# Forgetting attention: one f32 score product against three products of rounded high and low parts

## The reference

```python
q = rms_norm(q.reshape(B, S, FOX_HEADS, FOX_DH), q_norm_g)
k = rms_norm(k.reshape(B, S, FOX_HEADS, FOX_DH), k_norm_g)
log_f = jax.nn.log_sigmoid(f_raw.astype(F32) + b_f.astype(F32))
c = jnp.cumsum(log_f, axis=1)
# per block of 128 queries, q scaled by Dh ** -0.5:
logits = jnp.einsum('bhtd,bshd->bhts', qb, kf) + cb[..., None] - c_t[:, :, None, :]
logits = jnp.where(key_pos[None, :] <= q_pos[:, None], logits, -jnp.inf)
probs = jax.nn.softmax(logits, axis=-1)
o = jnp.einsum('bhts,bshd->bthd', probs, vf)
```

## Time and profile before

| | |
|---|---|
| median of 3 runs | 1759.19 us (1757.87 to 1759.38) |
| span of the profiled execution | 1755.8 us |
| TensorE busy | 1687.5 us, 96% |
| its weight loads | 1287.9 us, 73% |
| VectorE busy | 882.0 us, 50% |
| ScalarE busy | 788.9 us, 45% |
| GpSimd busy | 312.6 us, 18% |

### The profile page before, as it was taken

How to read it: one execution, slowest core, us unless ns; L and a number is a source line. 1 busy time by engine, 2 the same in 40 slices (tenths; PEclk the granted TensorE clock), 3 DMA queues, 4 the chain that set the end, 5 groups by cost and what they waited for, 6 DMA issues and landing times. The chain is left out here.

```text
span 1755.8 us, 28773 instructions
## 1 busy us (share of the span) xinstructions
PE 1687.5 (96%) x11157; PEld 1287.9 (73%) x11157; DVE 882.0 (50%) x1655; ACT 788.9 (45%) x1288; POOL 312.6 (18%) x243
## 2 busy tenths in 40 slices
PE   9999999999999899799999999999999999899898
PEld 6777777777777677678777887666666665688686
DVE  5757667575666635854322200344444544577533
ACT  4746556464554722142222311556555665531411
POOL 5213212132222251300000000222221221013000
PEclk9999999999999999999989999999999999999999
DMA  6202011210102122051130202111111101051411
GB/s 158 62 26 49 13 50 22 52 37 25 50 13 57 41 97 72 13 168 46 39 110 26 71 2 45 40 45 31 46 35 42 43 22 43 2 175 40 144 46 51
DMA packets 115574, 94.42 MB, mean 54 GB/s; under 512 B 19760, under 2 KB 97776, under 8 KB 115440
## 3 DMA queue, kind: packets, MB, share of 16 engines
q1 hardware_dynamic: 115440, 92.59, 18.5%
HBM read 84.08 MB, written 8.49 MB: 53 GB/s over the span
## 5 line engine op out<-in xcount | busy, mean ns | idle before, releaser
L435 PE MATMUL gdn_unit<-part_hi,gdn_w_hi 128*128 128x512 f32 x496 | 225.7, 455 | 0.0
L437 PE MATMUL gdn_unit<-part_hi,gdn_w_lo 128*128 128x512 f32 x496 | 195.3, 394 | 0.0
L436 PE MATMUL gdn_unit<-part_lo,gdn_w_hi 128*128 128x512 f32 x496 | 194.0, 391 | 0.0
L2108 DVE CUSTOM_DVE_ANT_0 fa_probs<-fa_scores,fa_decay 128x896 f32<-128x896 f32 (+7 forms) x128 | 97.0, 758 | 120.9 <-PE fa_scores L1920 73.6
L867 DVE SCALAR_TENSOR_TENSOR x<-gdn_raw,gdn_taps,x 128x512 f32<-128x512 f32 x144 | 129.4, 899 | 24.3 <-ACT x L665 19.4
L399 POOL TENSOR_TENSOR gdn_w_lo<-ring,gdn_w_hi 128x1024 fp32r<-128x1024 f32 x31 | 75.2, 2427 | 250.7 <-ACT gdn_w_hi L645 250.7
L2054 ACT ACTIVATE fa_probs_t<-fa_turned 128x512 f32<-128x512 f32 (+1 forms) x96 | 52.3, 545 | 139.0 <-PE fa_turned L1937 138.4
L2048 ACT ACTIVATE fa_probs<-fa_probs,fa_top 128x896 f32<-128x896 f32 (+7 forms) x128 | 99.4, 777 | 22.1 <-DVE fa_top L2108 18.4
L437 PEld LDWEIGHTS gdn_unit<-part_hi,gdn_w_lo 128*128 128x128 f32 x496 | 93.1, 188 | 21.0
L435 PEld LDWEIGHTS gdn_unit<-part_hi,gdn_w_hi 128*128 128x128 f32 x496 | 93.7, 189 | 16.1 <-issue 3.6
L1295 PE MATMUL e_gate<-e_w_hi,part_hi 128*128 128x512 f32 x256 | 101.8, 398 | 3.0 <-DVE part_lo L1430 2.8
(11 more groups left out here) (329 smaller groups left out, 3681.0 us busy)
## 6 DMA issues: line engine op xcount, KB each, us to landing
ring<-in_gdn_w_in_dram SPq DMA_DIRECT2D x31, 512.0 KB, 4.1
ring<-in_ple_w_gate_dram SPq DMA_DIRECT2D x32, 256.0 KB, 3.2
ring<-in_fox_w_in_dram SPq DMA_DIRECT2D x32, 256.0 KB, 3.1
ring<-in_fox_w_in_dram SPq DMA_DIRECT2D x16, 512.0 KB, 4.7
fa_decay<-c_rows_scratch SPq DMA_DIRECT2D x64, 128.0 KB, 3.0
gdn_g_bc<-g_rows_scratch SPq DMA_DIRECT2D x8, 512.0 KB, 8.9
x_scratch<-x SPq DMA_DIRECT2D x8, 512.0 KB, 2.9
m_old<-x_scratch SPq DMA_DIRECT2D x8, 512.0 KB, 3.5
```

Source lines behind the costliest of these rows:

```text
L435: pe.matmul(out, w_hi[:, j % 2, k, :], xh[:, k, ts], start=(k == 0), stop=False)
L436: pe.matmul(out, w_hi[:, j % 2, k, :], xl[:, k, ts], start=False, stop=False)
L437: mm = pe.matmul(out, w_lo[:, j % 2, k, :], xh[:, k, ts], start=False, stop=(k == KT - 1))
L2108: step(dve.tensor_tensor_reduce(probs[:, n % 3, blocks(e)], scores[head][:, blocks(e)], decay[:, head, blocks(e)], 1.0, 3e38, ALU.add, ALU ...
```

## The change

`qk` becomes single (T columns for keys, T for queries), and two tiles `qk_hi` and `qk_lo` of fp32r are added. Kind 0 is now the keys and kind 1 the queries, in the projection's weight columns, the prefetch and the gains. ScalarE copies the normalised values rounded into `qk_hi` (`split`), VectorE subtracts (`low_part`) into `qk_lo`. The queries are handled in two parts, the last 128 columns (the block of e = 0) first and the other 896 after. The scores are three fp32r products: high by high, high by low, low by high. `take_unit` waits until the split of what it overwrites is done. The DMA scratch size of the program is set to 1024.

```diff
-        qk = sb("qk", [P, 2, 2, T])
+        qk = sb("qk", [P, 2, T])
+        qk_hi, qk_lo = sb("qk_hi", [P, 2, T], F32R), sb("qk_lo", [P, 2, T], F32R)
...
+        def parts(kind):
+            return (slice(0, T),) if kind == 0 else (slice(T - P, T), slice(0, T - P))
...
         def columns(j):
-            pair, kind = j // 2, j % 2
-            return slice(kind * WIDTH + pair * P, kind * WIDTH + (pair + 1) * P)
+            pair, at = j // 2, (1 - j % 2) * WIDTH
+            return slice(at + pair * P, at + (pair + 1) * P)
...
             def score(p, e):
                 n, i = 2 * NT * p + 2 * e, row(e)
-                if e == 0:
-                    pe.wait_ge(normed, 2 * p + 2)
-                else:
+                if e:
                     pe.wait_ge(topped, n)
-                width = (i + 1) * P
+                pe.wait_ge(split_low, 3 * p + min(e, 1) + 2)
+                width, own = (i + 1) * P, slice(i * P, (i + 1) * P)
                 for at in range(0, width, HALF):
                     end = min(width, at + HALF)
-                    for head in range(2):
-                        rows = slice(head * DH, (head + 1) * DH)
-                        mm = pe.matmul(scores[head][:, at:end], qk[rows, p % 2, 0, i * P:(i + 1) * P],
-                                       qk[rows, p % 2, 1, at:end], start=True, stop=True)
-                        if end == width:
-                            mm.then_inc(scored, 1)
+                    for term, (a, b) in enumerate(((qk_hi, qk_hi), (qk_hi, qk_lo), (qk_lo, qk_hi))):
+                        for head in range(2):
+                            rows = slice(head * DH, (head + 1) * DH)
+                            mm = pe.matmul(scores[head][:, at:end], a[rows, 1, own], b[rows, 0, at:end],
+                                           start=(term == 0), stop=(term == 2))
+                            if end == width and term == 2:
+                                mm.then_inc(scored, 1)
...
             def take_unit(it, u):
                 n = 4 * it + u
                 act.wait_ge(unit_made, n + 1)
+                if it:
+                    act.wait_ge(split_low, 3 * it - (2 if u < 2 else 0))
...
+            def split(p, kind, part):
+                n, ts = kind + part, parts(kind)[part]
+                act.wait_ge(normed, 3 * p + n + 1)
+                if p:
+                    act.wait_ge(scored, 2 * NT * p)
+                step(act.activation(qk_hi[:, kind, ts], qk[:, kind, ts], ACT.Copy), split_high)
...
                     root(p, 0)
                     root(p, 1)
+                    split(p, 0, 0)
+                    split(p, 1, 0)
+                    split(p, 1, 1)
                 fill(AHEAD_OF_SCORES)
...
+            def normalise(p, kind, part):
+                ts = parts(kind)[part]
+                dve.wait_ge(roots, 2 * p + kind + 1)
+                step(dve.scalar_tensor_tensor(qk[:, kind, ts], qk[:, kind, ts], gains[:, kind:kind + 1],
+                                              squares[kind][:, ts], ALU.mult, ALU.mult), normed)
+
+            def low_part(p, kind, part):
+                n, ts = kind + part, parts(kind)[part]
+                dve.wait_ge(split_high, 3 * p + n + 1)
+                step(dve.tensor_tensor(qk_lo[:, kind, ts], qk[:, kind, ts], qk_hi[:, kind, ts].bitcast(F32),
+                                       ALU.subtract), split_low)
...
-                for kind in range(2):
-                    dve.wait_ge(roots, 2 * p + kind + 1)
-                    step(dve.scalar_tensor_tensor(qk[:, p % 2, kind], qk[:, p % 2, kind], gains[:, kind:kind + 1],
-                                                  squares[kind], ALU.mult, ALU.mult), normed)
+                normalise(p, 0, 0)
+                normalise(p, 1, 0)
+                low_part(p, 0, 0)
+                low_part(p, 1, 0)
+                normalise(p, 1, 1)
+                low_part(p, 1, 1)
...
-        to_attention = ahead("fa", columns(fox_in, (0, WIDTH)))
+        to_attention = ahead("fa", columns(fox_in, (WIDTH, 0)))
...
-    nc = _bacc.Bacc("TRN2", target_bir_lowering=False, num_devices=1)
+    nc = _bacc.Bacc("TRN2", target_bir_lowering=False, num_devices=1, dynamic_dma_scratch_size=1024)
```

## The result

The changed kernel takes 1770.85 us (median of 4 runs, 1769.6 to 1771.69) against 1759.22 before: a ratio of 1.0072, 95% interval 1.0058 to 1.0086. That is slower by 11.6 us; the forecast was 1770.2. The profiled execution has a span of 1769.1 us instead of 1755.8.

A forecast was written before the change was run, and what follows sets the result against it. TensorE's in-order queue, with its waits, was taken to bound the attention phase. Six middle pairs at +1.26 (+7.6), first +1.53 and last +1.9 summed to +11.0 on the 1759.19 median: 1770.2 us, range 1760.5 to 1784.

The forecast's parts named there:

- The score products: Attention scores: three fp32r products replace one f32, gaining 0.35 us in block e = 0 and 0.89 in e = 1 to 7.
- the wait for the bank: Behind block e = 0, TensorE's next triple waits until 1275.45 for ScalarE to empty the projection's single bank.
- the heads run side by side: Score products: forecast assumed both heads run together; rival that fp32r heads do not: 37 us more, 1807, chance 0.07.
- Narrow products: 128-key score parts: forecast 0.32 us, load-bound, instead of 0.213; rival at f32 price: 5.1 us more, 1775.3, chance 0.2.
- a middle pair: Each of six middle pairs of heads: two waits, 1.07 and 1.08, less 0.89 from the products, +1.26 us.
- Loads behind products: Score weight loads hide behind products of the same rows; rival that fp32r loads don't: 44 us more, 1814, chance 0.03.
- The first wait: Ahead of the first scores: TensorE waits for the split of keys and first queries, +1.07 us a middle pair.
- The second wait: Behind e = 0: late maxima on VectorE start e = 1 after 5.95 us instead of 4.86, +1.08 a pair.
- The exponentials' cover: Behind e = 0: exponentials start at 1277.3 instead of 1275.03 but end before their first reader; uncovered, some tenths.
- The last pair: Last pair of heads: start +1.34, e = 1 after 5.95 instead of 4.67, later blocks give back some 0.7: +1.9 us.
- The clock: Around e = 0 in each pair: rival that idle TensorE's clock falls to half, +12 us, 1782, chance 0.08.

The follow-up runs named there:

- e2: Changed kernel with three fp32r products per head but no split, the normalisations writing rounded values and low parts left out: 1746.51 us, ratio 0.9933.
- e3: Changed kernel with ScalarE taking the next pair's projection out of its bank ahead of copying the 896 query columns: 1771.21 us, ratio 1.0072.
- e8: The changed kernel measured again, without alteration, on another chip: 1768.1 us, ratio 1.0059.
- e7: Changed kernel with keys split in halves, last query subtraction on GpSimd, bank taken earlier, weights' subtraction later, last pair filled: 1755.06 us, ratio 0.9982.

## Why the prediction was right

Point by point, by its own steps.

- **The score products.** Forecast gain 1.24 a pair; e2 shows 1.32. e2 leaves the splits out; in the changed kernel itself the gain of e = 0 goes into the wait for the bank. The records are 576, in twos: the heads run side by side in fp32r too. Block e = 0 took 1.59 (forecast 1.57), e = 1 1.43 (1.40).
- **Narrow products.** The parts of 128 keys follow neither the column rate nor four cycles a column, but the load's bound: the weight loads come in pairs 0.11 us apart (1294.51 and 1294.62). In block e = 3 of the changed kernel the three products of 128 keys start 0.06 and 0.11 apart:

```profile
1294.28 0.39 PE L1926 MATMUL fa_scores<-fa_qk_hi,fa_qk_lo 64*128 64x512 f32 x2
1294.51 0.22 PE L1926 MATMUL fa_scores<-fa_qk_hi 64*128 64x128 f32 x2
1294.57 0.28 PE L1926 MATMUL fa_scores<-fa_qk_lo,fa_qk_hi 64*128 64x128 f32 x2
1294.68 0.28 PE L1926 MATMUL fa_scores<-fa_qk_hi,fa_qk_lo 64*128 64x128 f32 x2
1294.88 3.46 PE L1956 MATMUL fa_result<-fa_probs_t,x 128*64 128x256 f32 x32
```

  The first of them hides its load behind the product of 512, so only two of the three pay the 0.11. I had put 0.11 for each. So block e = 3 took 1.17 us, a gain of 0.11 instead of 0.07. Block e = 7 came out even instead of losing 0.11, and not by a cheap product: from its start to the next product of TensorE it takes 0.64 us in both kernels, where the forecast had some 0.42 before (0.213 on a floor of 0.21). Behind it stands `weigh`, which waits for VectorE's copy of the block before. That copy ends 0.10 ahead of it in both kernels (1316.44 + 0.56 = 1317.00 here, 1312.51 against 1312.61 before), so by these times the price of e = 7 is covered:

```profile
1316.44 0.56 DVE L2147 COPY fa_probs_t<-fa_turned 128x384 f32<-128x384 f32 x1
...
1317.10 1.26 PE L1956 MATMUL fa_result<-fa_probs_t,x 128*64 128x256 f32 x9
```

  Blocks e = 1 to 7 gave back 1.02 instead of 0.89, and that term, mis-sized by 0.13 (0.11 of it an overlap at e = 7 that the forecast had overlooked), is why a middle pair cost +1.15 and not +1.26.
- **Loads behind products.** They hide, also for fp32r products that follow one another on the same rows (0.23 to 0.24 a product at 512 columns, each with a load of its own: the high part of the queries twice, then the low). The rule of the Trainium skill ("TensorE: Matmul & The Clock Gate", Part 3, what overlaps and what doesn't), that a load overlaps only products of another row group, does not hold in this trace.
- **The first wait.** Forecast 1.07 over the kernel before in a middle pair; the chain from the second root's end (1273.16) to the scores (1275.96) takes 2.80, forecast 2.79, and 1.74 before: +1.06. (The forecast's own times, 1272.63 - 1271.58, give 1.05, not 1.07.) In the first pair the start moved by 1.36, forecast 1.34.
- **The second wait.** Forecast 5.95 from e = 0 to e = 1, measured 5.95; and that the maxima bind and the bank's wait only hides under them, which the changed kernel's own profile can't show, is what e3 showed. The bank was closer behind than forecast: 0.1 us instead of 0.4 (1278.2 and 1278.58).
- **The exponentials' cover** held: over the phase the transposes' products waited 2.7 us for them, 2.9 before.
- **The last pair.** Forecast +1.28 from e = 0 to e = 1 and -0.7 in the later blocks; e8 shows 5.95 - 4.67 = +1.28 and, 46.15 - 45.62 being +0.53, -0.75.
- **The clock** was a rival for every pair (+12). In the middle pairs it held at 1.00 with 0.97 and 1.28 us of idle time, so that rival fell. In the last pair, where nothing fills the two longer idle stretches, it fell in one of two profiles of this kernel; it cost 2.4 us there, 1.5 of it in block e = 1. The forecast had no term for it. Its hit within a microsecond is therefore partly luck: the sum was some 0.7 too high in the schedule (11.0, measured 1.36 + 8.39 + 0.53 = 10.3), and the clock, where it falls, adds more than that. The same kernel measured again (e8) came out 10.0 over the kernel before, under the forecast, and not over it. The row of the last pair before the change, 1.00 us idle at full clock, had been read as a cover; that the change more than doubles this stretch deserved a term with a chance of its own.

## What to carry to other kernels

When an edit puts a chain of small operations ahead of a critical product, follow the same engines' queues behind it too: here half the cost lay in the work that the later part of the split pushed back. The profile put all the idle time behind e = 0 down to the bank. But the way through the bank and the triples ended within 0.1 us of the maxima, and taking the bank's wait away alone brought nothing. Before cutting an operation in two to have its first part early, look for idle holes of the engine between the parts: filling the holes (one whole normalisation) gave back the whole loss. And an idle, slow engine can take work off the critical one: GpSimd's subtraction takes twice as long and still ended in time. How much of e7's gain is its own was not measured.

## What the runs showed of the hardware

The heads' products on different rows run side by side for fp32r as for f32: a pair of 512-column products every 0.23 to 0.24 us (1276.30 to 1276.54), against 0.43 for each of the two passes of f32.

The same program, with the same 2.3 and 2.2 us of TensorE idle in its last pair, kept the full clock (2.4 GHz) in one profile (e8) and fell to 1.2 GHz in block e = 1 in another. At the fallen clock the paired products of 512 columns came 0.42 to 0.43 us apart:

```profile
1501.77 0.80 PE L1926 MATMUL fa_scores<-fa_qk_hi 64*128 64x512 f32 x2 [2.25 <-DVE fa_top L2140]
1502.36 0.63 PE L1926 MATMUL fa_scores<-fa_qk_lo,fa_qk_hi 64*128 64x512 f32 x2
1502.78 0.63 PE L1926 MATMUL fa_scores<-fa_qk_hi,fa_qk_lo 64*128 64x512 f32 x2
```
